# The distance modulo 512 bytes between streamed activations and weights in a two-block fp32 kernel

## The chip, the core and the metric

The kernel runs on one core of one Trainium2 chip. The time is device microseconds from launch to end, the median of three runs; lower is better. TensorE multiplies a stationary operand (the weights, loaded by a weight-load instruction, LDWEIGHTS in the trace) with a moving operand (here the activations, streamed column by column). Both are read from SBUF, where a tile of [128, n] floats takes 4n bytes in each of 128 partitions at one byte offset. This case is about that offset.

## What is computed

A hybrid block (a modulated RMS norm, an input projection, a gated delta-net scan and a state-space scan over 256 latent and 256 context tokens, an output projection, a gated residual) is followed by a block of two layers, each with attention beside a short convolution and an MLP. All is fp32, width 2048, 256 tokens in the second block. What takes the time are the projections:

```python
u_l = rms_norm(h_lat, pre_w) * (1 + scale_l[:, None]) + shift_l[:, None]
z_l, xbc_l, dt_l, qkv_l, b_l, a_l = _split_proj(u_l @ w_in)
...
for l in range(DEPTH_2):
    h = _rmsnorm(x, attn_norm_g[l])
    ...
    x = x + jnp.concatenate([attn, conv.astype(attn.dtype)], axis=-1) @ w_out[l]
    hm = _rmsnorm(x, mlp_norm_g[l]) @ w_up[l]
    x = x + jnp.square(jax.nn.relu(hm)) @ w_down[l]
```

## The kernel before

**Units.** The weights come as a stream of 1 MB units, [128, 2048] floats each: 128 output features by 2048 inputs. The sync queue loads a unit into one of four buffers `raw0..3`; ScalarE casts it to the reduced format `fp32r` as `w_hi` (`split_act`, L417), VectorE subtracts to get the rest `w_lo` (`split_dve`, L424). Each has two slots in turn, and a third, spare slot (`w_spare`, L363 and L364) that four units use: `U_LAYER + 1`, `U_LAYER + 3` and, in each layer, the third unit of the output projection. The activations are split the same way into a high and a low part.

**The matmuls.** `unit_mm` (L430) does one unit: for each of 16 blocks of 128 inputs three matmuls, w_hi with low (L443), w_lo with high (L444), w_hi with high (L445), each with its own weight load of 128 columns. They stream T = 512 columns (latent and context tokens) or L = 256. Nearly every other operation only feeds this chain.

**The stages in time.** Adaptive modulation and the first units, 0 to 130 us; eight delta-net heads with projections of u laid between the small matmuls of the scan (to about 590); eight state-space tiles, likewise (to about 757); the output projection W_OUT, 16 units (to about 860). Then per layer eight heads of six units that stream h; 16 units of the output projection that stream a (1159 to 1251 us and 2237 to 2329 us); and the MLP in four parts, 64 "up" units that stream h and 64 "down" units that stream a, in the order of `MLP_ORDER` (L126).

**The tiles.** One arena of 53200 floats a partition is laid out by hand with `put` (L256), which allots tiles one behind the other or at a given byte. `raw`, `w_hi` and `w_lo` are 8 + 4 tiles of 8192 bytes and fill the first 65536 bytes, so that every slot starts at 0 modulo 512. Then:

```python
SKEW = 48
top["at"] += 4 * SKEW
a_hi = put("a_hi", KT * T, F32R)
a_lo = put("a_lo", KT * T, F32R)
...
top["at"] = shared
h_hi = put("h_hi", KT * L, F32R)
h_lo = put("h_lo", KT * L, F32R)
```

`a_hi`, `a_lo` hold u (the modulated input of block one), then the scans' output y, then in each layer the mixed heads and two quarters of the MLP's hidden values; `h_hi`, `h_lo` hold the normed activations. `SKEW` sets a at 192 modulo 512; `shared` is at 192 modulo 512 too. `bias` (attention bias) and `gate_raw` (four of the modulation's units) share the storage of a. `cs` is a small table used in the first block. Which engine waits for what is set by semaphores, none of which the change touches.

Of the kernel before, what the change touches and what calls it, by code (L numbers as in the profile page):

```python
# [69 lines left out]
SKEW = 48  # L70
# [175 lines left out]
def build(nc, stream, x_dram, const_dram, bucket_dram, par_dram, rel_dram, out_dram, scratch):  # L246
    ctx = ExitStack()
    with ctx:
# [109 lines left out]
        bias = put("bias", 2 * HEADS * L, at=4 * (RAW * D + 2 * SPL * D + SKEW + KT * L))  # L358
# [3 lines left out]
        gate_raw = [put(f"gate_raw{k}", D, at=4 * (RAW * D + 2 * SPL * D + SKEW + KT * T + KT * L + k * D)) for k in range(2)]  # L362
        for w, g in ((w_hi, 0), (w_lo, 1)):  # L363
            w.append(put(f"w_spare{g}", D, F32R, at=4 * (RAW * D + 2 * SPL * D + SKEW + KT * T + KT * L + g * D)))  # L364
# [124 lines left out]
        def diagonals(h0, h1):  # L489

            n = 2 * (h1 - h0)
            return (d3(bias[:, 2 * L * h0:2 * L * h1], L),
                    bass.AP(scratch[1].tensor, P - 1, [[PERIOD - 1, P], [P * PERIOD, n], [1, L]]))
# [32 lines left out]
        def _(sp):  # L526
# [33 lines left out]
            for begin, end in ((FIRST // RAW + 1, U_BC // RAW), ((U_LAYER + 12) // RAW, N_SEQ // RAW)):  # L560
# [7 lines left out]
                if end == U_BC // RAW:  # L568
# [26 lines left out]
                    for n in range(U_WOUT + 6, (U_LAYER + 12) // RAW * RAW):  # L595
                        sp.wait_ge(lo_ready, n - RAW + 1 - FIRST)
                        load(n, n % RAW)
                        if n == U_WOUT + 9:
                            sp.wait_ge(S["y_ready"], 7)
                            sp.dma_start(d3(x_res[:], L), x_dram[:, 0:L].rearrange("(k p) t -> p k t", p=P)).then_inc(S["x_loaded"], 16)  # L600
                        if n == U_LAYER + 10:
                            sp.wait_ge(S["bias_table"], 64)
                            sp.dma_start(scratch[1], bias[:]).then_inc(S["rel_out"], 16)
# [102 lines left out]
        def _(pe):  # L706
# [345 lines left out]
            mixed_order = [*range(8, KT), *range(8)]  # L1052
            quarters = (S["y_ready"], {8: 1, 12: 2, 0: 3, 4: 4, 5: 5, 6: 6, 7: 7})
# [37 lines left out]
            def first_normed(u, e, second=None):  # L1091

                ready = (S["h_ready2"], {k: (e - 1) * KT + k + 1 for k in range(KT)})
# [14 lines left out]
            for l in range(LAYERS):  # L1108
                base = U_LAYER + l * N_LAYER

# [75 lines left out]
                for kind, q in MLP_ORDER:  # L1186
                    if kind == "up":
                        hi, lo = h_hi3, h_lo3
                    else:
                        pe.wait_ge(S["mlp_ready"], (l * FQ + q + 1) * KT + 2)  # L1190
                        hi, lo = (a[:, (q % 2) * KT * L:(q % 2 + 1) * KT * L].rearrange("p (k t) -> p k t", t=L)
                                  for a in (a_hi, a_lo))
# [11 lines left out]
        def _(act):  # L1204
# [147 lines left out]
            def high(k):  # L1352
# [3 lines left out]
                for v in range(2):  # L1356
                    x = slice(k * T + v * L, k * T + (v + 1) * L)
                    m = f(a_hi[:, x], xr[:, x], ACT.Identity, bias=mods[:, 2 * k + v:2 * k + v + 1])
# [113 lines left out]
            def y_high(k0, k1):  # L1472

                act.copy(a_hi[:, k0 * L:k1 * L], x_res[:, k0 * L:k1 * L]).then_inc(S["y_hi"], 1)
# [76 lines left out]
            def weighted_hi(m, i, j):  # L1551
# [4 lines left out]
                act.mul(h_hi[:, tile], x_res[:, tile], par(name, i * 4 + (l * KT + j))).then_inc(S["h_hi_ready"], 1)  # L1556
# [4 lines left out]
            for l in range(LAYERS):  # L1561
# [13 lines left out]
                if l:  # L1575

                    act.dma_start(bias[:], scratch[1]).then_inc(S["bias_ready"], 16)
# [7 lines left out]
                def conv_high(i, j):  # L1585
                    act.wait_ge(S["conv_f32"], at(i, j))
                    act.copy(a_hi[:, ds(i * (2 * L) + (HEADS + j) * L, L)], b_co[:]).then_inc(S["conv_hi"], 1)
# [9 lines left out]
                def av_hi(i, j):  # L1597
                    act.wait_ge(S["attn_f32"], at(i, j))
                    act.copy(a_hi[:, ds(i * (2 * L) + j * L, L)], b_o[:]).then_inc(S["attn_hi"], 1)
# [46 lines left out]
                for kind, q in MLP_ORDER:  # L1646
                    def turn_(i, j):
                        u = Unit(c + j, i)
                        if kind == "up":
# [4 lines left out]
                            act.copy(a_hi[:, ds(tile, L)], hbuf[:, (2 + j % 2) * L:(3 + j % 2) * L]).then_inc(S["hi_relu"], 1)  # L1654
# [8 lines left out]
        def _(dve):  # L1663
# [67 lines left out]
            def low(k):  # L1731

                dve.wait_ge(S["u_hi"], k + 1)
                for v in range(2):
                    x = slice(k * T + v * L, k * T + (v + 1) * L)
                    m = stt(a_lo[:, x], xr[:, x], mods[:, 2 * k + v:2 * k + v + 1], a_hi[:, x], ALU.add, ALU.subtract)
# [232 lines left out]
            def y_low(k0, k1, n):  # L1969
# [3 lines left out]
                tt(a_lo[:, x], x_res[:, x], a_hi[:, x], ALU.subtract).then_inc(S["y_ready"], 1)  # L1973
# [135 lines left out]
            def weighted_lo(m, i, j):  # L2109
# [4 lines left out]
                stt(h_lo[:, tile], x_res[:, tile], par(name, i * 4 + (l * KT + j)), h_hi[:, tile], ALU.mult, ALU.subtract  # L2114
# [22 lines left out]
            for l in range(LAYERS):  # L2137
# [9 lines left out]
                def conv_low(i, j):  # L2147
                    dve.wait_ge(S["conv_hi"], at(i, j))
                    y = ds(i * (2 * L) + (HEADS + j) * L, L)
                    tt(a_lo[:, y], b_co[:], a_hi[:, y], ALU.subtract).then_inc(S["yt_ready"], 1)  # L2150

                def attn_low(i, j):
                    dve.wait_ge(S["attn_hi"], at(i, j))
                    y = ds(i * (2 * L) + j * L, L)
                    tt(a_lo[:, y], b_o[:], a_hi[:, y], ALU.subtract).then_inc(S["yt_ready"], 1)

                def head(i, j):
# [33 lines left out]
                    b = bias[:, ds(i * (4 * L) + j * 2 * L, 2 * L)]  # L2191
# [52 lines left out]
                for kind, q in MLP_ORDER:  # L2244
                    def turn_(i, j):
                        if kind == "up":
# [7 lines left out]
                            tt(a_lo[:, tile], hbuf[:, (2 + j % 2) * L:(3 + j % 2) * L], a_hi[:, tile], ALU.subtract  # L2254
# [112 lines left out]
```

## Time and profile before

| | us |
|---|---|
| median of three runs | 3031.68 (3027.84 to 3032.13) |
| span of the profiled execution | 3030.7 |
| TensorE matmuls busy | 2988.4 (99%) |
| TensorE weight loads busy | 2825.7 (93%) |
| VectorE busy | 1853.3 (61%) |
| ScalarE busy | 1333.4 (44%) |
| GpSimd busy | 192.4 (6%) |
| bytes moved by DMA | 547 MB, 181 GB/s in the mean |

The page of the profile gives busy time and counts by engine, the chain of work that ended last, and groups of instructions by source line. Matmuls are pipelined: the recorded duration of one (276 ns and more) is longer than the distance from its start to the next one's start, and it is the latter that adds up. The granted clock of TensorE is 1.00 of full speed in nearly all of the span.

### The profile page before, as it was taken

To read this page: it belongs to the slowest core of one execution; us is meant where nothing else is said; L and a number is where in the kernel's file an instruction comes from. 1 tells how busy PE (TensorE), PEld (TensorE's weight loads), DVE (VectorE), ACT (ScalarE), POOL (GpSimd) and SP (SyncE) were. 2 spreads that over 40 slices of the span, in tenths; PEclk is the share of its full clock that TensorE was granted. 3 is DMA by queue.
4 is the path that set the end of the run, shared out by engine and by line. 5 is a ranking of instruction groups with operands and counts; after the bars stand their busy time and mean duration, and the time that the engine had idled before them with its cause. 6 is when DMAs were issued, how large, how long until landed. Compare 5 with 4: busy or idle time off the path is not lost.

```text
span 3030.7 us, 68077 instructions
## 1 busy us (share of the span) xinstructions
PE 2988.4 (99%) x28670; PEld 2825.7 (93%) x28670; DVE 1853.3 (61%) x2510; ACT 1333.4 (44%) x1731; POOL 192.4 (6%) x287
## 2 busy tenths in 40 slices
PE   5999999999999999999999999999999999999999
PEld 2688888888999999999999999999999999999999
DVE  3677777688876666555455555566665555555554
ACT  3455555455454444444343333444444443333333
POOL 0000000000100001110010000100012110000000
PEclk8999999999999999999999999999999999999999
DMA  9712212323955444555555555544445555555554
GB/s 392 280 58 85 85 58 85 117 100 113 392 196 202 175 179 171 191 194 193 191 193 192 192 193 194 221 178 170 177 170 187 192 192 194 193 193 194 194 194 152
DMA packets 82964, 547.13 MB, mean 181 GB/s; under 512 B 9125, under 2 KB 13365, under 8 KB 18928
## 3 DMA queue, kind: packets, MB, share of 16 engines
q1 hardware_dynamic: 78448, 523.27, 47.1%
q10 hardware_dynamic: 2192, 15.40, 1.3%
q0 software_dynamic: 2160, 6.05, 0.6%
q8 instruction: 130, 2.13, 0.3%
q14 instruction: 34, 0.28, 0.0%
HBM read 540.46 MB, written 7.36 MB: 181 GB/s over the span
## 4 chain that ended last, share of the span: by engine, by line
PE 96%; DVE 1%; DMA 1%; PEld 0%; ACT 0%; issue 0%; PEldq 0%; SPq 0%; ACTq 0%; DVEq 0%
PE bank L443 29%; PE bank L444 28%; PE bank L445 28%; PE bank L845 1%; PE bank L712 1%; PE bank L718 1%; DMA raw<-stream 1%; PE bank L948 1%; PE bank L754 1%; DMA xr<-x_t 1%; PE bank L1150 0%; PE bank L770 0%; PE bank L931 0%; PE bank L771 0%; PE bank L772 0%; PE bank L956 0%
## 5 line engine op out<-in xcount | busy, mean ns | idle before, releaser
L422 ACT CAST w_hi<-raw 128x2048 fp32r<-128x2048 f32 x443 | 846.7, 1911 | 1226.3 <-PE bank L445 1226.2
L427 DVE TENSOR_TENSOR w_lo<-raw,w_hi 128x2048 fp32r<-128x2048 f32 x443 | 1017.6, 2297 | 550.7 <-ACT w_hi L422 550.6
L443 PE MATMUL bank<-a_lo,w_hi 128*128 128x256 f32 (+1 forms) x3568 | 1061.1, 297 | 0.6 <-DVE w_lo L2078 0.3
L444 PE MATMUL bank<-a_hi,w_lo 128*128 128x256 f32 (+1 forms) x3568 | 1035.5, 290 | 0.0
L445 PE MATMUL bank<-a_hi,w_hi 128*128 128x256 f32 (+1 forms) x3568 | 1035.2, 290 | 0.0
L443 PE MATMUL bank<-h_lo,w_hi 128*128 128x256 f32 x3552 | 990.5, 279 | 3.8 <-DVE h_lo L2114 3.8
L444 PE MATMUL bank<-h_hi,w_lo 128*128 128x256 f32 x3552 | 981.6, 276 | 0.0
L445 PE MATMUL bank<-h_hi,w_hi 128*128 128x256 f32 x3552 | 981.4, 276 | 0.0
L443 PEld LDWEIGHTS bank<-a_lo,w_hi 128*128 128x128 f32 x3568 | 672.0, 188 | 24.6 <-DVE g_X L1884 2.8
L445 PEld LDWEIGHTS bank<-a_hi,w_hi 128*128 128x128 f32 x3568 | 671.3, 188 | 17.2
L444 PEld LDWEIGHTS bank<-a_hi,w_lo 128*128 128x128 f32 x3568 | 670.9, 188 | 12.2
L443 PEld LDWEIGHTS bank<-h_lo,w_hi 128*128 128x128 f32 x3552 | 667.7, 188 | 5.0 <-issue 4.4
L444 PEld LDWEIGHTS bank<-h_hi,w_lo 128*128 128x128 f32 x3552 | 667.6, 188 | 0.9 <-issue 0.2
L445 PEld LDWEIGHTS bank<-h_hi,w_hi 128*128 128x128 f32 x3552 | 667.4, 188 | 0.0
L2229 DVE TENSOR_TENSOR x_res<-x_res,bank 128x256 f32 (+1 forms) x160 | 67.3, 421 | 190.8 <-PE bank L445 190.8
L703 POOL TENSOR_TENSOR hbuf<-hbuf 128x256 f32<-128x256 f32 x128 | 78.6, 614 | 967.7 <-DVE hbuf L2249 967.7
L2249 DVE SCALAR_TENSOR_TENSOR hbuf<-bank,n_rs 128x256 f32<-128x256 f32 x128 | 54.3, 425 | 114.3 <-PE bank L445 114.3
L685 POOL TENSOR_TENSOR n_sq<-x_res 128x256 f32 (+1 forms) x48 | 29.5, 614 | 852.2 <-DVE x_res L2229 851.2
L1673 DVE SCALAR_TENSOR_TENSOR g_acc<-g_pad,pars,g_acc 128x520 f32<-128x520 f32 (+1 forms) x112 | 74.4, 664 | 4.0
L1279 ACT COPY g_X<-bank 128x64 f32<-128x64 f32 x64 | 10.5, 217 | 125.6 <-PE bank L845 125.6
L754 PE MATMUL bank<-raw,c 128*32 128x512 f32 x256 | 36.5, 665 | 17.8 <-DMA raw<-stream 17.4
L2254 DVE TENSOR_TENSOR a_lo<-hbuf,a_hi 128x256 f32 x128 | 53.6, 418 | 0.0
(353 smaller groups left out, 2128.5 us busy)
## 6 DMA issues: line engine op xcount, KB each, us to landing
raw<-stream SPq DMA_DIRECT2D x485, 1024.0 KB, 4.8
gate_raw<-stream ACTq DMA_DIRECT2D x12, 1024.0 KB, 7.6
xr<-x_t SPq DMA_DIRECT2D x4, 1024.0 KB, 16.4
q_raw<-stream SPq DMA_DIRECT2D x8, 512.0 KB, 10.0
x_res<-x_t SPq DMA_DIRECT2D x1, 2048.0 KB, 16.2
bias_table<-bias SPq DMA_DIRECT2D x1, 2048.0 KB, 10.9
bias<-bias_table ACTq DMA_DIRECT2D x1, 2048.0 KB, 10.8
out_t<-x_res SPq DMA_DIRECT2D x4, 512.0 KB, 5.1
```

The source lines that it names most:

```text
L422: act.copy(w_hi[u.slot][:], raw[u.raw][:]).then_inc(hi_ready, 1)
L427: dve.tensor_tensor(w_lo[u.slot][:], raw[u.raw][:], w_hi[u.slot][:], ALU.subtract).then_inc(lo_ready, 1)
L443: pe.matmul(acc, wh, lo[:, k, 0:n], start=(k == first), stop=False)
L444: pe.matmul(acc, wl, hi[:, k, 0:n], start=False, stop=False)
L445: last = pe.matmul(acc, wh, hi[:, k, 0:n], start=False, stop=(k == final))
L703: pool.tensor_tensor(s, t, t, ALU.mult).then_inc(S["sq_relu"], 1)
L712: last = mm(psum[bank][:, at + n * w:at + (n + 1) * w], lhs, rhs, start=True, stop=True)
L754: m = mm(psum[6 + g % 2][t * B32:(t + 1) * B32, :], c32[:, (q * 4 + t) * B32:(q * 4 + t + 1) * B32], raw[n % RAW][:, t * 512:(t + 1) * 512 ...
L1673: m = stt(acc[:, 0:n], pad[:, k:k + n], weight(k), acc[:, 0:n], ALU.mult, ALU.add)
L2229: m = tt(x, x, psum[u.bank][:, 0:L], ALU.add)
L2249: stt(hbuf[:, (j % 2) * L:(j % 2) * L + L], psum[u.bank][:, 0:L], 0.0, n_rs[:], ALU.max, ALU.mult).then_inc(S["relu_ready"], 1)
L2254: tt(a_lo[:, tile], hbuf[:, (2 + j % 2) * L:(3 + j % 2) * L], a_hi[:, tile], ALU.subtract).then_inc(S["mlp_ready"], 1)
```

## The change

Each activation buffer gets names of its own for each stage, at other byte offsets within the same storage; a small gap is opened for it by moving `cs` to the end of the arena and the tiles behind `h_lo` by 512 bytes. u moves to 320 modulo 512; a to 256 (W_OUT and layer 0) and 224 (layer 1); h to 448, 384, 160 and 64 in its four stages (before attention and before the MLP, layer 0, then layer 1). The spare weight slot and the buffers `gate_raw`, which share its place, move from 192 to 0. Everywhere else the names follow; the instructions, their order and their waits stay.

```diff
-SKEW = 48
+U_SKEW = 320
+A_SKEW = (256, 224)
+H_SKEW = (448, 384, 160, 64)
...
-        top["at"] += 4 * SKEW
-        a_hi = put("a_hi", KT * T, F32R)
-        a_lo = put("a_lo", KT * T, F32R)
-        cs = put("cs", 2 * KT)
-        top["at"] += 4 * (P - SKEW - 2 * KT)
+        A0 = top["at"]
+        u_hi, u_lo = (put(n, KT * T, F32R, at=A0 + U_SKEW + 4 * KT * T * k) for k, n in enumerate(("u_hi", "u_lo")))
+        a_hi, a_lo = ([put(n, KT * T, F32R, at=A0 + skew + 4 * KT * T * k) for skew in A_SKEW] for k, n in enumerate(("a_hi", "a_lo")))
+        top["at"] += 4 * (P + 2 * KT * T)
+        cs = put("cs", 2 * KT, at=4 * (53200 - T - HALF - 2 * KT))
...
-        h_hi = put("h_hi", KT * L, F32R)
-        h_lo = put("h_lo", KT * L, F32R)
+        H0 = shared - 192
+        h_hi, h_lo = ([put(n, KT * L, F32R, at=H0 + max(skew, 192 + (skew - 192) % 512) + 4 * KT * L * k) for skew in H_SKEW]
+                      for k, n in enumerate(("h_hi", "h_lo")))
+        top["at"] += 4 * (2 * KT * L + P)
...
-            w.append(put(f"w_spare{g}", D, F32R, at=4 * (RAW * D + 2 * SPL * D + SKEW + KT * T + KT * L + g * D)))
+            w.append(put(f"w_spare{g}", D, F32R, at=X_RES - 4 * (2 - g) * D))
...
-        u_hi3, u_lo3 = (a[:].rearrange("p (k t) -> p k t", t=T) for a in (a_hi, a_lo))
-        y_hi3, y_lo3 = (a[:, 0:KT * L].rearrange("p (k t) -> p k t", t=L) for a in (a_hi, a_lo))
-        h_hi3, h_lo3 = (a[:].rearrange("p (k t) -> p k t", t=L) for a in (h_hi, h_lo))
+        u_hi3, u_lo3 = (a[:].rearrange("p (k t) -> p k t", t=T) for a in (u_hi, u_lo))
+
+        def mixed3(l):
+
+            return (a[l][:, 0:KT * L].rearrange("p (k t) -> p k t", t=L) for a in (a_hi, a_lo))
+
+        def normed3(m):
+
+            return (a[m][:].rearrange("p (k t) -> p k t", t=L) for a in (h_hi, h_lo))
```

## Rows read from the trace of the kernel before

**Rows 1.** The page: busy us by engine; the chain by engine
```profile
PE 2988.4 (99%) x28670; PEld 2825.7 (93%) x28670; DVE 1853.3 (61%) x2510; ACT 1333.4 (44%) x1731; POOL 192.4 (6%) x287
PE 96%; DVE 1%; DMA 1%; PEld 0%; ACT 0%; issue 0%; PEldq 0%; SPq 0%; ACTq 0%; DVEq 0%
```

**Rows 2.** Windows: us, busy us (count) by engine, clock, DMA share, GB/s
```profile
1251.00:1957.00 706.00, 706.00 (x6223) 705.79 (x6222) 380.00 (x341) 278.45 (x217) 61.42 (x98) 1.00 0.54 193
```

**Rows 3.** Windows: MLP and output projection, all engines; then both projections, TensorE alone
```profile
1256.00:1800.00 544.00, 544.00 (x4802) 544.00 (x4801) 292.74 (x264) 211.06 (x165) 39.57 (x65) 1.00 0.53 193
1182.00:1250.00 68.00, 68.00 (x580) 68.00 (x579) 38.09 (x37) 27.77 (x24) 16.22 (x24) 1.00 0.52 186
...
1165.00:1251.00 86.00, 86.00 (x730) 1.00 0.51 184
2244.00:2333.00 89.00, 89.00 (x757) 1.00 0.52 187
```

**Rows 4.** Timeline of TensorE, spare slot, five starts left out: start us, us, line, operands
```profile
888.76 0.28 PE L445 MATMUL bank<-h_hi,w_spare 128*128 128x256 f32 x1
...
889.49 0.28 PE L445 MATMUL bank<-h_hi,w_spare 128*128 128x256 f32 x1
```

**Rows 5.** By form, L444: whole span; 1400 to 1800; 1182 to 1250; 889 to 893
```profile
L444 PE MATMUL bank<-a_hi,w_lo 128*128 128x256 f32 x3184 | 883.8, 278 | 0.0
...
L444 PE MATMUL bank<-a_hi,w_lo 128*128 128x256 f32 x588 | 162.3, 276 | 0.0
...
L444 PE MATMUL bank<-a_hi,w_lo 128*128 128x256 f32 x193 | 54.2, 281 | 0.0
...
L444 PE MATMUL bank<-h_hi,w_spare 128*128 128x256 f32 x12 | 3.4, 283 | 0.0
```

**Rows 6.** Tile w_spare (ns min/median/max), and the page's lines of ordinary splits
```profile
L444 PE MATMUL bank<-h_hi,w_spare x32: 279/283/415, 861.2 to 893.0; 128*128 128x256 f32 x32
L422 ACT CAST w_spare<-raw x4: 1892/1902/1906, 851.3 to 2245.8; 128x2048 fp32r<-128x2048 f32 x4
L427 DVE TENSOR_TENSOR w_spare<-raw,w_spare x4: 2285/2292/2293, 853.4 to 2247.7; 128x2048 fp32r<-128x2048 f32 x4
...
L422 ACT CAST w_hi<-raw 128x2048 fp32r<-128x2048 f32 x443 | 846.7, 1911 | 1226.3 <-PE bank L445 1226.2
L427 DVE TENSOR_TENSOR w_lo<-raw,w_hi 128x2048 fp32r<-128x2048 f32 x443 | 1017.6, 2297 | 550.7 <-ACT w_hi L422 550.6
```

**Rows 7.** Timeline of TensorE in W_OUT, with one- and two-column matmuls
```profile
804.49 0.28 PE L443 MATMUL bank<-a_lo,w_hi 128*128 128x256 f32 x1
...
804.72 0.28 PE L445 MATMUL bank<-a_hi,w_hi 128*128 128x256 f32 x1
...
805.20 0.36 PE L1071 MATMUL bank<-keep,gate_acc 128*128 128x1 f32 x2
...
805.65 0.36 PE L1071 MATMUL bank<-keep,gate_acc 128*128 128x1 f32 x2
```

**Rows 8.** Timeline of TensorE, 512 columns
```profile
702.37 0.39 PE L444 MATMUL bank<-a_hi,w_lo 128*128 128x512 f32 x1
...
703.07 0.39 PE L444 MATMUL bank<-a_hi,w_lo 128*128 128x512 f32 x1
```

**Rows 9.** Timeline of TensorE around two sum matmuls
```profile
1164.90 0.47 PE L443 MATMUL bank<-a_lo,w_hi 128*128 128x256 f32 x1
1165.21 0.28 PE L444 MATMUL bank<-a_hi,w_lo 128*128 128x256 f32 x1
...
1254.33 0.59 PE L1085 MATMUL bank<-n_acc,keep 128*128 128x256 f32 x2
1254.76 0.59 PE L1088 MATMUL bank<-n_sq,keep 128*128 128x256 f32 x2
1255.00 0.47 PE L443 MATMUL bank<-h_lo,w_hi 128*128 128x256 f32 x1
1255.31 0.28 PE L444 MATMUL bank<-h_hi,w_lo 128*128 128x256 f32 x1
```

More of the change, by code:

```diff
@@ L354, in build @@
         top["at"] = shared
-        h_hi = put("h_hi", KT * L, F32R)
-        h_lo = put("h_lo", KT * L, F32R)
+        H0 = shared - 192
+        h_hi, h_lo = ([put(n, KT * L, F32R, at=H0 + max(skew, 192 + (skew - 192) % 512) + 4 * KT * L * k) for skew in H_SKEW]
+                      for k, n in enumerate(("h_hi", "h_lo")))
+        top["at"] += 4 * (2 * KT * L + P)
         mo = put("mo", KT * L, at=shared + 4 * KT * L)
-        bias = put("bias", 2 * HEADS * L, at=4 * (RAW * D + 2 * SPL * D + SKEW + KT * L))
+        bias = [put("bias", 2 * HEADS * L, at=A0 + skew + 4 * KT * L) for skew in A_SKEW]
         n_sq, n_acc, n_ln, n_rs = (put(n, L) for n in ("n_sq", "n_acc", "n_ln", "n_rs"))
@@ L361, in build @@
         small = put("small", 64)
-        gate_raw = [put(f"gate_raw{k}", D, at=4 * (RAW * D + 2 * SPL * D + SKEW + KT * T + KT * L + k * D)) for k in range(2)]
+        gate_raw = [put(f"gate_raw{k}", D, at=X_RES - 4 * (2 - k) * D) for k in range(2)]
         for w, g in ((w_hi, 0), (w_lo, 1)):
-            w.append(put(f"w_spare{g}", D, F32R, at=4 * (RAW * D + 2 * SPL * D + SKEW + KT * T + KT * L + g * D)))
+            w.append(put(f"w_spare{g}", D, F32R, at=X_RES - 4 * (2 - g) * D))
         gate_acc = put("gate_acc", 3 * 512, at=top["at"])
@@ L1555, in weighted_hi @@
                 tile = ds(i * (4 * L) + j * L, L)
-                act.mul(h_hi[:, tile], x_res[:, tile], par(name, i * 4 + (l * KT + j))).then_inc(S["h_hi_ready"], 1)
+                act.mul(h_hi[m][:, tile], x_res[:, tile], par(name, i * 4 + (l * KT + j))).then_inc(S["h_hi_ready"], 1)
             norm_root(0)
@@ L1653, in turn_ @@
                             tile = i * (4 * L) + ((q % 2) * KT + j) * L
-                            act.copy(a_hi[:, ds(tile, L)], hbuf[:, (2 + j % 2) * L:(3 + j % 2) * L]).then_inc(S["hi_relu"], 1)
+                            act.copy(a_hi[l][:, ds(tile, L)], hbuf[:, (2 + j % 2) * L:(3 + j % 2) * L]).then_inc(S["hi_relu"], 1)
                         elif not isinstance(i, int) or u.c + i * 4 + 2 < N_SEQ:
@@ L2113, in weighted_lo @@
                 tile = ds(i * (4 * L) + j * L, L)
-                stt(h_lo[:, tile], x_res[:, tile], par(name, i * 4 + (l * KT + j)), h_hi[:, tile], ALU.mult, ALU.subtract
+                stt(h_lo[m][:, tile], x_res[:, tile], par(name, i * 4 + (l * KT + j)), h_hi[m][:, tile], ALU.mult, ALU.subtract
                     ).then_inc(S["h_ready2"], 1)
@@ L2253, in turn_ @@
                             tile = ds(i * (4 * L) + ((q % 2) * KT + j) * L, L)
-                            tt(a_lo[:, tile], hbuf[:, (2 + j % 2) * L:(3 + j % 2) * L], a_hi[:, tile], ALU.subtract
+                            tt(a_lo[l][:, tile], hbuf[:, (2 + j % 2) * L:(3 + j % 2) * L], a_hi[l][:, tile], ALU.subtract
                                ).then_inc(S["mlp_ready"], 1)
```

31 lines of the change are left out of this document (17 added, 14 removed).

## The prediction

> **What bounds the kernel now.** I read the busy shares and the chain of work first: TensorE is busy 2988.4 of 3030.7 us and owns 96% of the chain [rows 1]. Then the stages by window: from 1251 to 1957 us TensorE has no gap at all, at full granted clock, while VectorE is busy 54% of the time, ScalarE 39% and the DMA engines 0.54 [rows 2]. So the time is a count of matmuls times the distance from one start to the next, and anything that alters this distance, which I call the rhythm, comes straight out at the end. The durations (276 ns and up) overlap and are no price by themselves; the starts are. In a window the count takes in two matmuls that began before it, so I take two off.
>
> The rhythm of the 256-column matmuls has three values in this trace, at one clock. In the MLP it is 544/4800 = 113.3 ns, for matmuls that stream a and for those that stream h alike (up and down units alternate there). In the output projection it is 68/578 = 117.6 ns [rows 3]. With the spare weight slot six starts take 0.73 us by rounded stamps, 120 to 122 ns each; I take 120 [rows 4]. The durations follow: 276 ns in the quick rhythm, 281 in the slow one, 283 with the spare slot [rows 5]. That gives a meter for stretches where starts are hard to count.
>
> Where do the operands stand? By the allocations the ordinary weight slots lie at 0 modulo 512 bytes (every buffer ahead of them is 8192 bytes long), a at 4*48 = 192, h at 192 as well, and the spare slot at 192. So distance (activation minus weights) is 192 nearly everywhere, and 0 with the spare slot. The change makes it 320 for u, 256 and 224 for a in layers 0 and 1 (256 for W_OUT too), 448, 384, 160 and 64 for h in the four normed stages, and puts the spare slot at 0.
>
> **Part by part.**
> *Nothing is added or removed* in any queue: no instruction, wait or DMA moves, no tile's size changes, and the aliases of a name overlap the same storage in other stages. Splits written at 192 instead of 0 cost the same: 4 ScalarE casts into the spare slot take a median of 1902 ns and 4 VectorE subtractions 2292, against means of 1911 and 2297 for ordinary slots [rows 6]. So ScalarE, VectorE and the moved table `cs` cost nothing; even if a write cost some ns more, VectorE's half-idle time covers it. All that remains is TensorE's rhythm.
>
> *The spare slot.* Each of the three lines has 32 matmuls on it with h [rows 6] and, for the third units of the two output projections, 32 with a: 192 in all. From 120 to 113.3 they give 192 x 6.7 ns = 1.3 us. Bounds: 0 (they merely take over the neighbours' rhythm) and 1.6 (192 x 8.3, down to the load bound below).
>
> *a and u, 256 columns.* The line that is never first after a break, L444, has 3184 such matmuls with a, 883.8 us in all, so 277.6 ns in the mean [rows 5]. Between 276.0 (quick, 162.3/588) and 280.8 (slow, 54.2/193) that is a share of 0.33 in the slow rhythm: 0.33 x 3 x 3184 = 3150 matmuls, each 4.4 ns long: 13.9 us. The two output projections hold 728 + 755 starts between 1165 and 1251 and between 2244 and 2333 [rows 3]; less 96 on the spare slot that is some 1390, or 6.1 us. The W_OUT units are slow too (804.49 to 804.72, two starts on) [rows 7]: 16 x 48, nearly all at full length, 3.0 us. The remaining 4.8 us lie in the scan stages before 752 us, where these matmuls fill the wait for VectorE and ScalarE. What a shorter filler returns there depends on which wait ends last, so I take half, 2.4 us.
>
> *u, 512 columns.* 24 units of 48, 1152 matmuls. Three starts take 0.70 us (702.37 to 703.07), 233 ns each [rows 8], while an fp32 record of a 256-column sum, which streams the same number of passes twice over, starts 215 ns after the one before it (0.43 us for two records) [rows 9]. So up to 18 ns each, 21 us, lie above the nearest plain streaming rate; below, nothing excludes a loss of equal sort. Nothing shows a distance at which they run faster; I take 0 and keep -10 and +5 us for the range, since half of them, too, fill waits.
>
> *h.* These run at 113.3 already and recover it after the break at 1254.76 [rows 3, 9]; I take 0. The floor is near: matmuls of one or two columns, which do nothing but load 128 weight columns, follow each other at 0.45/4 = 112 ns (805.20 to 805.65, two pairs) [rows 7]. So a full 256-column stream can win at most 1.6 ns each.
>
> **Does the distance set the rhythm?** For: the only matmuls at distance 0 are the slowest, 283 against 276 ns, and in the same windows. Against: distance 192 has both rhythms. Behind a sum matmul a restarts at 1164.90 with a first step of 0.31 us and goes on at 118 ns to the end of the stage; behind the sum matmul at 1254.76 h restarts with the same step of 0.31 us at the same distance, and the window from 1256 us on runs at 113.3 [rows 3, 9]. So the rhythm has a memory: perhaps two reads that walk through the same banks in step, entered at a break and kept. The distance should decide whether the longer rhythm is entered and can last. The trace says nothing of where it can.
> The Trainium skill (TensorE: Matmul & The Clock Gate, What happens when you issue a matmul) says that TensorE has two independent SBUF read ports and that loading the next weights takes no read bandwidth from the running matmul. By that rule no distance matters. The trace disagrees as far as the spare slot goes, 283 against 276 ns.
>
> **Sum of the forecast.** 1.3 + 6.1 + 3.0 + 2.4 = 12.8 us off the profiled span of 3030.7, which stands 1.0 us below the median of the runs. 3031.7 - 12.8 = 3018.9 us; I say 3019. Its own range, 3010 to 3026: down by part of the 512-column bound, up where one of the two larger stages stays slow.
>
> **Rivals.**
> *No change.* The 118 ns rhythm is entered by the timing of the break, whatever the distance; or the sites merely swap. Only the spare slot gains: 3030, range 3026 to 3036. For it: same distance, two rhythms. This is also what the rule of the read ports gives: 3031.7, no term at all.
> *Slower: a long stage falls into the 118 ns rhythm and keeps it.* The new distances are eight, the trace knows two, and one of those two is bad. The long stages are at the floor now, so they can only lose. It takes a distance that keeps the slow rhythm, as 192 does in the output projections [rows 3]. Each layer has 64 up and 64 down units; one such set is 64 x 48 = 3072 matmuls x 4.4 ns = 13.5 us. With all smaller gains kept, one set slow gives about 3032, two 3046, and one set with no gain elsewhere 3045. It is slower than before from the point where more than some 2900 matmuls (12.8/0.0044) turn slow. At the spare slot's 120 ns one set costs 20.6 us. Against it: h leaves the 118 ns rhythm by itself at 192, so it isn't very sticky. I put this at 3042.
> *Faster still: everything drops to the load bound.* About 20,400 matmuls of 256 columns less the 3150 at 118 ns and 192 on the spare slot, some 17,000 at 1.6 ns or less, give up to 27 us; with the forecast and a further 5 us of the 3150 that is about 2986. For it: transposes and one-column loads do run at 112. Against: a and h, different lines, different loops, all show 113.3 exactly.
> The Trainium skill (same page, Back-to-back issue gap) gives 262 cycles for 256 columns, an estimate of 109.2 ns and some 80 us less in all; the one-column row of 112 ns speaks against it, since every matmul here loads its own weights.
>
> **How the numbers follow.** Forecast 0.46; no change 0.22; slower 0.20; load bound or a large part of it 0.12. A measurement of this kernel can tell about 0.2%, 6 us, from no change. Faster: 0.46 + 0.12 = 0.58; same 0.22; slower 0.20. For the range, 3000 to 3043: the low end takes the forecast with the full 10 us of the 512-column term and part of the load-bound case, and leaves out 0.09; the high end takes one set slow at 3042 and leaves out 0.10.
>
> **What would show it.** If right: by-form mean of L444 with a and 256 columns falls from 277.6 to about 276; 1182 to 1250 holds about 602 matmuls instead of 580; the spare rows show 276; the MLP windows still 113.3. The end of each stage moves forward by the terms above and MLP lengths don't change. If an MLP window shows 281 ns durations, the slower rival holds; if L444 stays at 277.6, no change. I am wrong if the distances have modes of their own that 192 doesn't show, above all in the h stages, where I price nothing.

## The result, and the profile after

The changed kernel takes 3107.78 us (3107.39 to 3108.17), the kernel before 3030.19 in the same comparison: a ratio of 1.0259, 95% interval 1.0247 to 1.0272. It is 78 us slower where 13 us less were forecast, and outside the range.

The work is the same and the clock is the same. The page of the changed kernel, whose span is 3105.9 us, by engine (it answers [rows 1]):

```profile
PE 3064.5 (99%) x28670; PEld 2903.4 (93%) x28670; DVE 1855.2 (60%) x2510; ACT 1331.9 (43%) x1731; POOL 192.3 (6%) x287
```

Its costliest groups of TensorE, forms kept apart (for [rows 5]; line, operands, count | busy us, mean ns | idle):

```profile
L448 PE MATMUL bank<-h_hi,w_lo 128*128 128x256 f32 x3552 | 993.0, 280 | 0.0
L448 PE MATMUL bank<-a_hi,w_lo 128*128 128x256 f32 x2784 | 785.2, 282 | 0.0
L448 PE MATMUL bank<-u_hi,w_lo 128*128 128x512 f32 x384 | 150.3, 392 | 0.0
```

TensorE's count is unchanged to the instruction, and its busy time is 76.1 us longer, while VectorE and ScalarE moved by 2 us and less. The extra time is in the matmuls themselves. Windows of TensorE alone (us, busy us (count), clock, DMA share, GB/s) show it stage by stage, in this order: output projection and MLP of layer 0 (up parts, then down parts, the last of these long), then the up and down parts of layer 1:

```profile
1180.00:1248.00 68.00, 68.00 (x569) 1.00 0.51 186
1256.00:1430.00 174.00, 174.00 (x1468) 1.00 0.51 186
1440.00:1520.00 80.00, 80.00 (x669) 1.00 0.51 181
1810.00:1980.00 170.00, 170.00 (x1419) 1.00 0.51 182
2380.00:2550.00 170.00, 170.00 (x1445) 1.00 0.52 185
2930.00:3090.00 160.00, 160.00 (x1355) 1.00 0.51 180
```

With the two matmuls that began before a window taken off: matmuls with a at 256 start every 170/1417 = 120.0 ns, with h at 384 every 174/1466 = 118.7, with h at 64 every 170/1443 = 117.8, with a at 224 every 160/1353 = 118.3. All of these were at 113.3 before, in layer 0 by [rows 3] and in layer 1 by these windows of an up and a down part of the kernel before (155/1368 and 160/1413):

```profile
2340.00:2495.00 155.00, 155.00 (x1370) 1.00 0.54 192
2855.00:3015.00 160.00, 160.00 (x1415) 1.00 0.53 190
```

The output projection was at 117.6 before and is at 68/567 = 119.9 now. Only attention of layer 0, h at 448, kept its old rhythm; attention of layer 1, h at 160, went from 276 to 280 ns a matmul. The group of h_hi by w_lo in a window of that stage, of the kernel before (L444 there is the same source line):

```profile
L444 PE MATMUL bank<-h_hi,w_lo 128*128 128x256 f32 x714 | 197.3, 276 | 0.0
```

And of the changed kernel:

```profile
L448 PE MATMUL bank<-h_hi,w_lo 128*128 128x256 f32 x692 | 193.9, 280 | 0.0
```

The sum closes. Each up or down set of a layer is 3072 matmuls: down of layer 0 6.7 ns each, 20.6 us; up of layer 0 5.4, 16.6; down of layer 1 5.0, 15.4; up of layer 1 4.5, 13.8. Attention of layer 1 is 2304 matmuls at some 4 ns, 9. These make 75.4 us. The two projections add 2.1, and everything up to the second use of the spare slot is 2.4 us shorter (the unit ahead of it starts at 881.0 us before and at 878.6 now). The two spans differ by 75.2 us.

### The profile page after: what moved, and what is told of

Its sections match the earlier page's. It is cut to its first block, busy times and chain, and to the rows that moved or that the text cites. A ratio compares the mean times of both kernels' runs of the same rounds, so it can differ in the third digit from the quotient of the medians.

```text
span 3105.9 us, 68077 instructions
## 1 busy us (share of the span) xinstructions
PE 3064.5 (99%) x28670; PEld 2903.4 (93%) x28670; DVE 1855.2 (60%) x2510; ACT 1331.9 (43%) x1731; POOL 192.3 (6%) x287
## 4 chain that ended last, share of the span: by engine, by line
PE 95%; DVE 2%; DMA 1%; PEld 0%; ACT 0%; issue 0%; PEldq 0%; SPq 0%; ACTq 0%; DVEq 0%
PE bank L447 29%; PE bank L449 28%; PE bank L448 28%; PE bank L855 1%; DMA raw<-stream 1%; PE bank L728 1%; PE bank L722 1%; PE bank L958 1%; DMA xr<-x_t 0%; DVE g_L L1857 0%; PE bank L1163 0%; PE bank L764 0%; PE bank L941 0%; DVE g_X L1878 0%; PE bank L780 0%; PE bank L966 0%
## 5 line engine op out<-in xcount | busy, mean ns | idle before, releaser
L447 PE MATMUL bank<-a_lo,w_hi 128*128 128x256 f32 x2784 | 786.5, 282 | 0.1
L449 PE MATMUL bank<-a_hi,w_hi 128*128 128x256 f32 x2784 | 785.2, 282 | 0.0
L448 PE MATMUL bank<-a_hi,w_lo 128*128 128x256 f32 x2784 | 785.2, 282 | 0.0
L447 PEld LDWEIGHTS bank<-a_lo,w_hi 128*128 128x128 f32 x2784 | 529.9, 190 | 2.1 <-issue 1.7
L447 PE MATMUL bank<-u_lo,w_hi 128*128 128x256 f32 (+1 forms) x784 | 287.1, 366 | 0.6 <-PEq L466 0.3
L449 PE MATMUL bank<-u_hi,w_hi 128*128 128x256 f32 (+1 forms) x784 | 262.7, 335 | 0.0
L448 PE MATMUL bank<-u_hi,w_lo 128*128 128x256 f32 (+1 forms) x784 | 261.9, 334 | 0.0
L447 PEld LDWEIGHTS bank<-u_lo,w_hi 128*128 128x128 f32 x784 | 147.4, 188 | 21.8 <-DVE g_X L1897 3.7
L449 PEld LDWEIGHTS bank<-u_hi,w_hi 128*128 128x128 f32 x784 | 147.1, 188 | 16.4
L448 PEld LDWEIGHTS bank<-u_hi,w_lo 128*128 128x128 f32 x784 | 147.9, 189 | 11.6
```

What stands on the lines that cost most here:

```text
L447: pe.matmul(acc, wh, lo[:, k, 0:n], start=(k == first), stop=False)
L448: pe.matmul(acc, wl, hi[:, k, 0:n], start=False, stop=False)
L449: last = pe.matmul(acc, wh, hi[:, k, 0:n], start=False, stop=(k == final))
```

## The experiments

All use the changed kernel's code unless said otherwise, so that a distance is one number for each stage. Diffs show the numbers that changed against it. "Only a back", "Only a changed", "Move both", the sweep, "Between the steps", "High and low parts apart" and "Only w_lo moved" were executed once each; their readings rest on windows of the trace more than on the one time.

**Undo all distances.** Is it the distances, or anything else in the rewrite?

```diff
-U_SKEW = 320
-A_SKEW = (256, 224)
-H_SKEW = (448, 384, 160, 64)
+U_SKEW = 192
+A_SKEW = (192, 192)
+H_SKEW = (192, 192, 192, 192)
```

> The changed kernel with every distance set back to 192 (u, a in both layers, h in all four stages); the spare weight slot stays at 0 modulo 512 and the neighbours stay where the change put them. Distance theory (the rhythm of a stage is set by activation minus weight slot modulo 512): MLP windows back at 113.3 ns a matmul, output projections 117.6, time 3029 us (that of before less up to 1.3 us for the spare slot). Rival (something else in the rewrite costs the time: the moved neighbours, the aliases, the spare slot): stays near 3108.

3022.78 us in the median of ten executions (3020.6 to 3025.1), ratio to the kernel before 0.9978 (0.9968 to 0.9987). The whole loss is gone while the moved neighbours stayed where the change had put them, so it is the distances. It also lies 6 us below the 3029 that was expected. Windows of TensorE in the output projections of both layers and in the first up and down parts:

```profile
1180.00:1246.00 66.00, 66.00 (x584) 1.00 0.53 191
1256.00:1420.00 164.00, 164.00 (x1449) 1.00 0.53 192
1430.00:1505.00 75.00, 75.00 (x664) 1.00 0.53 190
2255.00:2320.00 65.00, 65.00 (x576) 1.00 0.55 196
```

The MLP is back at 164/1447 = 113.3 ns, and the projections run at 66/582 = 113.4 instead of 117.6 [rows 3]. This is the forecast's own gain for the projections, with a left at 192; of the tiles that they use, only the spare slot stands elsewhere than before.

**Only a back to 192.**

```diff
-A_SKEW = (256, 224)
+A_SKEW = (192, 192)
```

> Only a goes back to 192 in both layers; u 320 and h 448, 384, 160, 64 stay changed. Each stage by its own distance: the a stages return to 113.3 (down units) and about 117.6 (projections), the up units stay at 118.7 in layer 0 and 117.8 in layer 1, attention of layer 1 at 118.0; a gain of 20.4 + 1.6 + 15.4 + 0.5 us, and some 2 in W_OUT, so about 3068. Inheritance theory (h is at 118 because each up part follows a down part that ran long and the rhythm is carried over): h stages fall back to 113.3 as well, about 3035.

3078.34 us, 10 us above the first theory and far above the second. Windows: projection, up, down, down and down (the last) of layer 0; then projection and down of layer 1:

```profile
1180.00:1240.00 60.00, 60.00 (x512) 1.00 0.53 192
1250.00:1422.00 172.00, 172.00 (x1452) 1.00 0.51 184
1430.00:1512.00 82.00, 82.00 (x699) 1.00 0.51 184
...
1612.00:1690.00 78.00, 78.00 (x691) 1.00 0.53 190
...
1790.00:1950.00 160.00, 160.00 (x1414) 1.00 0.54 192
...
2275.00:2345.00 70.00, 70.00 (x620) 1.00 0.54 196
...
2535.00:2615.00 80.00, 80.00 (x681) 1.00 0.52 185
```

Neither theory as stated. h at 384 stays at 172/1450 = 118.6 ns: it has its length from its own distance, not from a. But a at 192 behind it runs at 82/697 = 117.6 in the first down part, at 78/689 = 113.2 in the second and at 160/1412 = 113.3 in the third, and in layer 1, behind h at 64 (117.8 ns), it runs at 80/679 = 117.8; the last and longest down part does too (160 us hold 1361, 117.7 ns). The carry-over exists, and it goes into a stage that stands at 192. The two projections differ as well, with the same distances: 60/510 = 117.6 ns in layer 0, 70/618 = 113.3 in layer 1.

**Only a changed**, the other half:

```diff
-U_SKEW = 320
-H_SKEW = (448, 384, 160, 64)
+U_SKEW = 192
+H_SKEW = (192, 192, 192, 192)
```

> Only a changed (256 for W_OUT and layer 0, 224 for layer 1), u and h at 192. Own prices from the stages of the changed kernel: W_OUT 3.6, projections 4.6 and 3.5, down parts 20.4 and 15.4, together 47.5 over 3022.8: 3070 us, with all up parts at 113.3 ns. Carry-over (at 192 the stream keeps the rhythm in which it was handed over, as a at 192 kept 117.8 behind h at 64 and 384): up parts 3 and 4, which follow a down part without a break, at 117.8, 3.4 us each and four of them: 3084 us; up parts 1 and 2, behind the sum matmul, at 113.3.

3072.77 us, so the stages' own prices, 3070, and not the carry-over. Windows: down of layer 0, then the up parts behind a down part in layers 0 and 1:

```profile
1435.00:1520.00 85.00, 85.00 (x711) 1.00 0.52 185
1530.00:1605.00 75.00, 75.00 (x665) 1.00 0.52 189
2635.00:2705.00 70.00, 70.00 (x620) 1.00 0.53 194
```

85/709 = 119.9 ns in the down part, 75/663 = 113.1 right behind it, without a break. Here a stream at 120 or 118.3 ns hands nothing on to a stage at 192. In the run before, one at 117.8 did in layer 1, and one at 118.7 did once of three times.

**Move both.** The first 65536 bytes hold four raw and four split slots of 8192 bytes each (not 8 + 4, as is said ahead of the prediction), so all of these stood at 0 modulo 512. Now the four split ones, the ordinary weight slots, go up by 64 bytes, and the activations stand 192 above them:

```diff
-U_SKEW = 320
-A_SKEW = (256, 224)
-H_SKEW = (448, 384, 160, 64)
+U_SKEW = 256
+A_SKEW = (256, 256)
+H_SKEW = (256, 256, 256, 256)
...
+        top["at"] += 64
         w_hi = [put(f"w_hi{s}", D, F32R) for s in range(SPL)]
         w_lo = [put(f"w_lo{s}", D, F32R) for s in range(SPL)]
+        top["at"] -= 64
```

> All weight slots but the spare one move by 64 bytes and u, a and h stand at 256 modulo 512: distance 192 everywhere, at other absolute offsets. Distance theory: 113.3 ns in the MLP, about 3030 us (the spare slot is at distance 256 now, +1). Absolute-place theory (an activation at 256 is bad whatever the weights do, for instance against other engines' accesses): 120 ns in all a and h stages, some 20,000 x 6.7 ns more, about 3150.

3029.14 us. The up parts hold 1450 matmuls in 164 us, 113.3 ns, with a and h at the offset 256 that gave a 120 ns. So it is the distance between activations and weight slots and not the place of either; raw buffers, psum and the small tiles stayed where they were. The output projection holds 538 in 63 us, 117.5 ns, with its spare slot at distance 256.

One rival is left by this: ScalarE and VectorE write the next unit's weights into such slots, at the same distance, while TensorE reads the activations. The trace of the changed kernel speaks against it. In a down part of layer 0, at distance 256, VectorE is busy 37.75 of 80 us and ScalarE 25.99, and yet every one of 223 matmuls of a line has the same 283 ns, and each start follows the one before it by 119 or 120 ns (window with all engines; shortest/median/longest):

```profile
1440.00:1520.00 80.00, 80.00 (x669) 80.00 (x669) 37.75 (x28) 25.99 (x15) 0.00 (x0) 1.00 0.51 181
L448 PE MATMUL bank<-a_hi,w_lo x223: 283/283/283, 1440.1 to 1520.0; 128*128 128x256 f32 x112
```

The spare slot says the same: while it was read at distance 0 before, at 120 ns, the splits went into ordinary slots at distance 192. What counts is the distance to the weights that TensorE itself reads. That the two reads disturb each other is the plainest reading; no record shows the reads.

**A sweep.** One distance a stage:

```diff
-U_SKEW = 320
-A_SKEW = (256, 224)
-H_SKEW = (448, 384, 160, 64)
+U_SKEW = 448
+A_SKEW = (448, 32)
+H_SKEW = (96, 448, 128, 288)
```

> A sweep, one distance a stage: u 448, a 448 (W_OUT and layer 0) and 32 (layer 1), h 96, 448, 128, 288. The changed kernel showed 113.6 ns at 448 in attention of layer 0 and 120.0 at 256, as 192 and 0 did before: if only the distance modulo 256 counts, 448 gives 113.3 in up and down units of layer 0 as 192 does, and 288 what 32 gives. If modulo 512 counts, 448 and 192, 288 and 32 differ. The other values are unknown: 116 to 120 by the five that were seen and were long. About 3070 in all.

3072.48 us. Windows: up (448), down (448), up (288), down (32):

```profile
1262.00:1430.00 168.00, 168.00 (x1481) 1.00 0.53 190
1440.00:1515.00 75.00, 75.00 (x664) 1.00 0.53 195
2365.00:2525.00 160.00, 160.00 (x1374) 1.00 0.51 186
2535.00:2615.00 80.00, 80.00 (x688) 1.00 0.52 189
```

The timeline with h at 96, two matmuls of one line that are six starts apart (start us, us, line, operands), 0.72 us for six, 120 ns each:

```profile
1004.10 0.29 PE L447 MATMUL bank<-h_lo,w_hi 128*128 128x256 f32 x1
...
1004.82 0.29 PE L447 MATMUL bank<-h_lo,w_hi 128*128 128x256 f32 x1
```

448 gives 75/662 = 113.3 ns, as 192. 288 and 32 give 160/1372 and 80/686, both 116.6. With 0 and 256 at 120 that is three pairs 256 bytes apart that agree: the distance counts modulo 256. The table is then complete in steps of 32:

| distance modulo 256 | ns a matmul, 256 columns | from |
|---|---|---|
| 0 | 120 | spare slot before, a at 256 |
| 32 | 116.6 | h at 288, a at 32 |
| 64 | 117.8 | h at 64 |
| 96 | 120 | h at 96 |
| 128 | 118.7 | h at 384 |
| 160 | 118.0 | h at 160 |
| 192 | 113.3 (or 117.7, below) | a and h at 192 and at 448 |
| 224 | 118.3 | a at 224 |

The value for 160 is the mean start distance in attention of layer 1 without the gaps; its units alternate between some 117.4 and 118.6, so it is the least steady one. The 512-column matmuls of u prefer another place: the middle line of a block takes 392 ns at 320 against 395 at 192 and 448, and 233 ns from start to start become 230.

**Between the steps.** Layer 0 at 176, layer 1 at 208 (a tile 16 bytes off its alignment is a slice of a slightly larger one):

```diff
-U_SKEW = 320
-A_SKEW = (256, 224)
-H_SKEW = (448, 384, 160, 64)
+U_SKEW = 352
+A_SKEW = (176, 208)
+H_SKEW = (176, 176, 208, 208)
```

> How wide is the good place: layer 0 (a and h) at 176, layer 1 at 208, u at 352. Known so far, modulo 256: 160 gives 118.0 ns, 192 gives 113.3, 224 gives 118.3. If what counts are pieces of 32 bytes, 176 reads across two of them and gives about 118, and 208 likewise; if the place is broader than 32 bytes both give 113.3; a value below 113.3 would show that 192 isn't the best. The load bound seen before is 112.

3134.48 us. 176 gives 170/1426 and 208 gives 175/1468, both 119.2 ns, worse than the steps on either side of them. So 16 bytes off the good place it is gone. Both tiles also lie off the 32-byte grid of all the others, and whether that or the distance makes them the worse, this run can't tell:

```profile
1275.00:1445.00 170.00, 170.00 (x1428) 1.00 0.52 182
...
2400.00:2575.00 175.00, 175.00 (x1470) 1.00 0.52 182
```

**High and low parts apart.** Who has to stand at 192? Each pair is (high part, low part).

```diff
-U_SKEW = 320
-A_SKEW = (256, 224)
-H_SKEW = (448, 384, 160, 64)
+U_SKEW = 32
+A_SKEW = ((256, 448), (192, 256))
+H_SKEW = ((256, 448), (256, 448), (192, 256), (192, 256))
```

> Two of the three matmuls of a block stream the high part. Layer 0: high part of a and h at 256, low part at 448; layer 1: high part at 192, low part at 256; u at 32. Theory one (each matmul pays for its own distance): layer 0 (2 x 120 + 113.3)/3 = 117.8 ns, layer 1 (2 x 113.3 + 120)/3 = 115.5. Theory two (the rhythm is one for the whole stream, and a single bad member puts it off the short one): both near 118 to 120. Theory three (only the high part's distance counts, since it is read beside both weight loads): layer 0 120, layer 1 113.3.

3114.34 us. Layer 0, with the high part at 256: 170/1444 = 117.7 ns. Layer 1, with two of three matmuls at 192 and the low part at 256: 170/1426 = 119.2 ns. The layer with more members at the good place is the longer one, which rules out both the price for each matmul and the high part alone.

```profile
1265.00:1435.00 170.00, 170.00 (x1446) 1.00 0.52 185
...
2385.00:2555.00 170.00, 170.00 (x1428) 1.00 0.52 182
```

**Only w_lo moved**, by 64 bytes, a and h at 192 (u, in its own stages, at 160):

```diff
-U_SKEW = 320
-A_SKEW = (256, 224)
-H_SKEW = (448, 384, 160, 64)
+U_SKEW = 160
+A_SKEW = (192, 192)
+H_SKEW = (192, 192, 192, 192)
...
         w_hi = [put(f"w_hi{s}", D, F32R) for s in range(SPL)]
+        top["at"] += 64
         w_lo = [put(f"w_lo{s}", D, F32R) for s in range(SPL)]
+        top["at"] -= 64
```

> All activations at 192, high weight slots at 0, low weight slots at 64 modulo 512, u at 160. w_lo is loaded while w_hi times low part streams, and streams (as stationary operand) in the next matmul. If the distance between the streamed operand and the weights loaded beside it counts, one matmul of three (the one beside the w_lo load) is at distance 128, which gave 118.7 alone: about 115 in the mean by own prices, 118 if the stream has one rhythm. Rival: only w_hi counts: 113.3.

3110.79 us; 170/1438 = 118.2 ns in an up part of layer 0, and the same in layer 1. One of the four tiles of the loop off its place costs nearly as much as distance 128 for all of them (118.7), and all three lines are longer than the 276 ns of the short rhythm. The spare slot, whose two halves stayed together at 0, is the control inside the same run. With a at 192 it takes 276 ns a matmul in the output projection, between units at 118 ns. A window of an up part of layer 0, and its three lines by form:

```profile
1265.00:1435.00 170.00, 170.00 (x1440) 1.00 0.52 185
L451 PE MATMUL bank<-h_hi,w_hi 128*128 128x256 f32 x480 | 135.6, 283 | 0.0
L449 PE MATMUL bank<-h_lo,w_hi 128*128 128x256 f32 x480 | 135.2, 282 | 0.0
L450 PE MATMUL bank<-h_hi,w_lo 128*128 128x256 f32 x480 | 134.2, 280 | 0.0
```

The tile view of the spare slot, one line's matmuls with a_hi (count: shortest/median/longest ns, first and last start):

```profile
L450 PE MATMUL bank<-a_hi,w_spare x32: 276/276/287, 1179.5 to 2303.8; 128*128 128x256 f32 x32
```

**The spare slot alone**, in the code of the kernel before (`cs` moves out of its way, `gate_raw` moves with the spare slot, in whose bytes it lies):

```diff
-        cs = put("cs", 2 * KT)
-        top["at"] += 4 * (P - SKEW - 2 * KT)
+        cs = put("cs", 2 * KT, at=4 * (53200 - T - HALF - 2 * KT))
+        top["at"] += 4 * (P - SKEW)
...
-            w.append(put(f"w_spare{g}", D, F32R, at=4 * (RAW * D + 2 * SPL * D + SKEW + KT * T + KT * L + g * D)))
+            w.append(put(f"w_spare{g}", D, F32R, at=X_RES - 4 * (2 - g) * D))
```

> The kernel before with one thing moved: the spare weight slot and gate_raw from 192 to 0 modulo 512 (and cs out of their way). If the spare slot at distance 0 is what keeps the output projections at 117.6 ns (the pause before it ends the long rhythm where the distance is 192, and can't where it is 0), both projections go to 88.8 us from 91.8, and the time is about 3023 as with all at 192 in the changed code: 0.2% under the kernel before. If the spare slot is worth only its own 192 matmuls: 1.3 us.

Seven of ten executions took 3021.6 to 3024.6 us, as expected. The other three took 3052.1 to 3053.9; the ratio over all of them is 1.0012 (0.9986 to 1.0038). The kernel before took 3028.3 to 3031.0 in all of 23 executions on that chip. Where the 7 us come from is seen at the third unit of the projection. Timeline of the kernel before, at the change to the spare slot:

```profile
1171.45 0.39 PE L443 MATMUL bank<-a_lo,w_spare 128*128 128x256 f32 x1
1171.68 0.28 PE L444 MATMUL bank<-a_hi,w_spare 128*128 128x256 f32 x1
...
1174.18 0.28 PE L444 MATMUL bank<-a_hi,w_spare 128*128 128x256 f32 x1
...
1174.90 0.28 PE L444 MATMUL bank<-a_hi,w_spare 128*128 128x256 f32 x1
```

The same place in the kernel with all at 192:

```profile
1170.40 0.39 PE L447 MATMUL bank<-a_lo,w_spare 128*128 128x256 f32 x1
1170.62 0.28 PE L448 MATMUL bank<-a_hi,w_spare 128*128 128x256 f32 x1
...
1171.09 0.28 PE L449 MATMUL bank<-a_hi,w_spare 128*128 128x256 f32 x1
...
1171.31 0.28 PE L448 MATMUL bank<-a_hi,w_spare 128*128 128x256 f32 x1
```

Both streams come in at 118 ns and pause for 0.2 us. At distance 0 the first goes on at 120 (0.72 us for six starts) and hands 117.6 to the 13 units behind it; at 192 the second is at 113 four matmuls later and stays there. It isn't always so at 192. Over the profiled executions of all runs, the projection of a layer with a at 192 or 448 came out of this pause in the short rhythm 14 times of 17 with the spare slot at the same distance, and 0 times of 6 with the spare slot at distance 0 or 256. The three that stayed long are layer 0 of "Only a back" (above) and one projection each in two runs below.

**u at 320, the rest at 192.** Can the two gains be had together?

```diff
-A_SKEW = (256, 224)
-H_SKEW = (448, 384, 160, 64)
+A_SKEW = (192, 192)
+H_SKEW = (192, 192, 192, 192)
```

> u 320 as in the changed kernel, everything else at 192, spare slot at 0. By the stages seen so far: the scan stages end 5 to 8 us earlier than with u at 192 (708.0 against 702.9 and 700.4 us from the first projection to the last u matmul), the rest as with all at 192 (3022.8 us): about 3016 us, 0.4 to 0.5% under the kernel before. Rival (the shorter 512-column matmuls only turn into waits of the scans, and W_OUT takes over a longer rhythm from u): 3020 to 3023.

Ten of twelve executions took 3018.7 to 3022.3 us, two 3050.4 and 3051.2; ratio 0.9987 (0.9965 to 1.001). The same kernel on another chip:

> The kernel with u at 320 and all else at 192 once more, on one chip with the kernel before with the spare slot moved: 3018 to 3021 us, 2 to 5 us less than with u at 192, from 512-column matmuls at 230 instead of 233 ns; if that is lost in waits, the same as the spare slot alone.

Three of twelve at 3020.0 to 3024.4, nine at 3048.9 to 3052.1; ratio 1.0043 (1.0019 to 1.0066). Its profiled execution is a long one. Windows: projection, up, last down of layer 0; projection and down of layer 1:

```profile
1180.00:1240.00 60.00, 60.00 (x512) 1.00 0.52 182
1255.00:1425.00 170.00, 170.00 (x1446) 1.00 0.51 186
...
1800.00:1960.00 160.00, 160.00 (x1361) 1.00 0.52 188
2270.00:2345.00 75.00, 75.00 (x663) 1.00 0.55 196
2530.00:2605.00 75.00, 75.00 (x664) 1.00 0.53 189
```

From the projection on, all of layer 0 runs at 117.6 to 117.8 ns, and the same stages of layer 1 at 113.3 to 113.5, with the same distances. The long rhythm, once it passes the pause at the spare unit and the sum matmul before the MLP, holds through the 13 units behind the spare one and the 128 of the MLP: 6768 matmuls at 4.4 ns are 30 us, the step between the two times.

**Is it the spare slot that keeps the kernel before out of this?** u 320, the rest and the spare slot at 192:

```diff
-A_SKEW = (256, 224)
-H_SKEW = (448, 384, 160, 64)
+A_SKEW = (192, 192)
+H_SKEW = (192, 192, 192, 192)
...
-            w.append(put(f"w_spare{g}", D, F32R, at=X_RES - 4 * (2 - g) * D))
+            w.append(put(f"w_spare{g}", D, F32R, at=X_RES - 320 - 4 * (2 - g) * D))
```

> u 320, everything else at 192, and the spare slot back at 192, which is distance 0, as in the kernel before. With the spare slot at 0 the same kernel took either 3020 or 3050 us: in the long case the 117.8 ns rhythm, entered in the output projection, went on through the sum matmul and all of a layer's MLP. If the spare units at distance 0 are what brings the stream to that sum matmul in a position from which it always returns to 113.3, no run is near 3050, both projections take 91.8 us, and the time is 3024 to 3026. If it is chance alone, runs near 3055 come up here as well.

3026.81 us (3025.3 to 3032.2), ratio 0.9994 (0.9985 to 1.0003), no execution near 3050 in 11, projection at 62/527 = 117.6 ns.

**And does it hang on 192 itself?** The same distances for u and all weight slots as in the changed kernel, a and h at 448, 256 bytes further than 192:

```diff
-A_SKEW = (256, 224)
-H_SKEW = (448, 384, 160, 64)
+A_SKEW = (448, 448)
+H_SKEW = (448, 448, 448, 448)
```

> u 320, a and h at 448, spare slot at 0: 448 is 192 plus 256. If only the distance modulo 256 counts, this is the kernel with 192 once more: 3018 to 3022 us in the short case, near 3050 in others. If the whole distance counts, the second time is absent or another.

3022.09 us (3019.8 to 3025.0), ratio 0.9976 (0.9967 to 0.9985), and none near 3050 in 11 either. So on this chip neither tells: without a second time at 448 the absence at distance 0 proves nothing. But the profile of the run at 448 has a projection in the long rhythm at 448 too. That of layer 1 has 64/544 = 117.6 ns, and the up part behind it 155/1368 = 113.3:

```profile
2252.00:2316.00 64.00, 64.00 (x546) 1.00 0.54 187
2335.00:2490.00 155.00, 155.00 (x1370) 1.00 0.53 191
```

So a long projection is not enough for a long MLP: here, and behind all six projections with the spare slot at distance 0 or 256, the MLP fell back to 113.3; behind the long one with u at 320 and the rest at 192 it did not. Side by side on one more chip, 192 and then 448:

> u 320, all else at 192, spare slot at 0, on one chip with the same kernel at 448. It took 3050 us in 2 of 12 executions on one chip and in 9 of 12 on another. If the second time hangs on the distance as a whole, some executions here are near 3050 and none of the kernel at 448 is.

> u 320, a and h at 448, spare slot at 0. It took 3020 to 3025 us in all of 11 executions. If only the distance modulo 256 counts, it shows times near 3050 as often as its neighbour at 192 does; if it is free of them here where the neighbour isn't, 448 is the better place.

At 192 one of six executions took 3019.5 us, four 3049.4 to 3051.7, one 3080.9; the mean of all six is 0.7% above that of the kernel before. At 448 five of twelve took 3019.1 to 3022.5, four 3050.3 to 3052.8, three 3079.1 to 3082.0; the mean of all twelve is 0.6% above. The expectation that 448 would be free of it fell: the distance counts modulo 256 in this too. The granted clock is the same 0.994 to 0.996 in all of these executions. A third time, one more step of 30 us, fits both layers being caught, which no profile here shows. How often it happens differs widely: with the spare slot at the same distance as the others (192 or 448) it was 0 of 10, 2 of 12, 3 of 10, 9 of 12, 0 of 11, 5 of 6 and 7 of 12, in the order of the runs. The kernel before ran beside all of them, 91 executions between 3027.4 and 3032.4 us, and never showed it. On the chip with 3 of 10 against 0 of 23 the two kernels differ in the places of the spare slot (with `gate_raw` in its bytes) and `cs` alone. That points to the old place of the spare slot as what keeps the kernel before out of it (or that of `cs`, which no matmul's rhythm hangs on as far as the runs show). By which step it does so is open: at distance 0 the projection is always long, and yet the MLP behind it always recovers.

## Why the prediction was wrong

**What held.** The bound (a count of matmuls times their start distance), the meter by durations (276, 281 and 283 ns answer to 113.3, 117.7 and 120; within 2 ns, for h at 64 has 279 at 117.8), no cost in any other engine, and that the long stages at 113.3 "can only lose". The slower rival had the right direction and nearly the right unit price, 13.5 us for a set of 3072 matmuls; measured were 13.8 to 20.6. Its mechanism was right in part: the stages didn't fall into the longer rhythm of 192 and keep it, each distance has a rhythm of its own. That is what the last sentence of the prediction named as the way to be wrong, "above all in the h stages, where I price nothing".

**The step that failed** is that the long stages at new distances were put at nothing. Under "h" it says "I take 0"; measured were 16.6 + 13.8 us for the up parts and some 9 for attention of layer 1. The down parts, which stream a, have no term at all (its signs have "the MLP windows still 113.3") and cost 20.6 + 15.4. With it went the gains where a's new distance was to end the slow rhythm: 6.1 us for the projections, 3.0 for W_OUT. The prediction priced the new distances at the best rhythm that the old one had shown. But of the two distances the trace knew, one was good part of the time and one bad always; the new ones (seven, where the prediction says eight) had nothing in their favour. The runs show that of eight places modulo 256 one is good. Of the seven stages' new distances only 448 is at that place. The text said that the trace "says nothing of where it can" last, and then gave 0.46 to the case where it lasts nowhere.

**The argument against the slower rival** was wrong as well: "h leaves the 118 ns rhythm by itself at 192, so it isn't very sticky". That is a property of 192. At 64, 160, 224, 256 and 384 there is no short rhythm to return to: no window of the changed kernel in these stages shows one. Even at 192 h doesn't always leave it: with u at 320 it once kept it through the MLP of layer 0. The rival was also too small. It let one set turn long, 3042 us; with no evidence for any distance all four sets and an attention stage had to be in its sum, 4 x 13.5 and 10 more, some 3095, and the range had to reach there.

**The memory** was seen rightly and its place partly missed. It exists where the distance is 192 modulo 256, and these runs show it only there. The spare slot was priced at its own 192 matmuls, 1.3 us; it decides for 13 units behind it and is worth 6 to 7 us, and with that the forecast's 6.1 us for the projections were to be had without moving a at all. That 6.1 us of the forecast turned to a loss of 2.1 at 256 and 224. W_OUT at 256 takes 99.2 us from the first to the last start of its middle line (753.4 to 852.6), with a at 192 and u at 320 it takes 95.2. The 2.4 us for u's 256-column fillers did not come: nearly all their units run at 119.6 to 121.8 ns a start before and after.

**The 512-column term** was taken as 0 with a bound of 10 us below: the stage gained 3 ns a matmul, and u at 320 is worth some 2 to 3 us (3020 against 3023 in the short case, on different chips), so the term was small, as was said.

**The load-bound rival** fell: no distance shows less than 113.3 ns. The 262 cycles that the prediction takes from the Trainium skill (TensorE: Matmul & The Clock Gate, Back-to-back issue gap) are given there for a matmul by itself, which no run here has.

The Trainium skill (SBUF — State Buffer, SBUF: two separate sides) says that on the engine side only the port pair shared by VectorE and GpSimd causes contention and that TensorE never waits on anyone. Nothing here contradicts that for other engines. But the byte distance between TensorE's two operands alone lengthens a start by up to 6.7 ns over 113.3. The rule of two independent read ports, cited ahead of the result, doesn't hold here in the sense that the prediction gave it, that no distance matters.

## What to carry to other kernels

Where matmuls with their own weight load follow each other without a gap, the byte distance between moving and stationary operand is a parameter worth 3 to 6% of their time. It must be measured for every stage and every slot, the rare ones too, and a place not measured should be priced at the mean of the known ones, not at the best. Count starts per window for each stage: the mean duration moves by only 3 to 7 ns, and the busy share of 99% doesn't move at all. Where one distance shows two rhythms, time it often and on more than one chip before a gain of 0.3% is believed.

No kernel here beats the one before with certainty. All at 192 with the spare slot at 0 took 0.2% less in all of 10 executions, but the same distances in the code of the kernel before gave the long time in 3 of 10. u at 320 with the rest at 192 or 448 takes 3020 us in its short case, 0.3% less, and 3050 or 3080 in others; with the spare slot at distance 0 it is steady in 11 executions on one chip and the same as before within 0.1%.

## What the runs showed of the hardware

- The rhythm of 256-column matmuls with 128 columns of weights each depends on the distance modulo 256 bytes: 113.3 ns at 192 (or 117.7, below), 116.6 to 120 ns in the other steps of 32, 119.2 at 176 and 208.
- It is one rhythm for the whole stream: one of four tiles 64 bytes off lengthens all three matmuls of the loop, from 113.3 to 118.2 ns in the mean of their starts.
- At 192 and at 448 there are two rhythms that keep themselves, 113.3 and 117.7 ns. Pauses can switch between them, and which one results isn't the same in each execution: steps of 30 us between executions of one kernel, at the same granted clock (0.993 to 0.997).
- 512-column matmuls prefer another distance: 230 ns at 320 against 233 at 192 and 448.
